# Constant products in TensorE's waits, maxima taken one head at a time, and the bias tables' flips between the turns of tiles

## The chip, the cores and the metric

The kernel runs on one core of a Trainium2 chip. The metric is the device time in microseconds of one execution, from its start to its end. A time of the kernel before is the median of three executions; the profile is of a further execution, which has a time of its own. Numbers of the trace are in microseconds (us) from the first instruction, unless they are marked ns. A few names recur. TensorE (PE) multiplies matrices; VectorE (DVE), ScalarE (ACT) and GpSimd (POOL) do the work by element; SyncE (SP) starts transfers. PEclk is the clock granted to TensorE as a share of full speed: 0.50 is 1.2 GHz and 1.00 is 2.4 GHz.

## The reference

Two transformer blocks in float32, one after the other, over 1024 tokens of width 1024 with 256 context tokens beside them. What bears on this case:

```python
# first block, two layers
h = rms_norm(x, norm_gain[l]) * (1 + scale) + shift          # also for the context tokens
z = h @ w_in[l]                                              # 22 tiles of 128 columns
a_out = global_gqa(aq, ak, av, ak_c, av_c)                   # dense softmax attention, 8 query heads of 64
b_out = pool_branch(bz, pool_w[l], pool_scale[l])
n_out = neighbourhood_attn(nq, nk, nv, nk_c, nv_c, na_rpb[l], rows)   # with a table of relative biases
x = x + gate * (concat(a_out * silu(ag), b_out * silu(bg), n_out * silu(ng)) @ w_out[l])
...
# second block, one layer
z = rmsnorm(x, g_mix) @ w_in
y_fox = softmax(q k^T + c_q - c_k, causal) @ v               # 8 heads of 64
y_rwkv = rwkv7_scan(...)                                     # a recurrence over the tokens
x = x + (gate_fox * (y_fox @ w_o_fox) + gate_rwkv * (y_rwkv @ w_o_rwkv)) @ w_out
x = x + (gelu(u1) * u2) @ w_down                             # u = conv(rmsnorm(x) @ w_up)
x = x + sigmoid(rmsnorm(x) @ w_ple_gate) * (p @ w_ple_up)
```

## The kernel before

Activations lie feature-major in SBUF, tiles of 128 features by 1024 (or 1280, with the context) tokens. A product is made from rounded parts: a weight and an operand are each split into a high and a low part, and three products (`w.hi` x `hi`, `w.hi` x `lo`, `w.lo` x `hi`) are added up in one bank of the accumulators. Weight tiles come one by one into a ring of two, and GpSimd splits each when the tile before it in its slot has been used (`part_weights`, L252 and L254; first two: L230 and L238, or `part_first`, L220 and L222).

The program is a row of sections with a barrier of all engines between them; inside a section each engine has its own list and waits on semaphores. The sections, with their place in the profiled span:

- `opening` and `project` for layer 0 (to 398 us) and layer 1 (1017 to 1329 us): the norm makes the operand tile by tile, k = 0 to 7, and TensorE multiplies two weight tiles with each as it comes (L1719 to L1721); then a chunk at a time. The third weight tile (j == 2) can be split only when the first two are through.
- `attention_operands` (399 to 426, 1330 to 1356 us): TensorE turns 30 tiles of values in 8 groups (L1128), ScalarE copies each group out (L1168); then it flips four bias tables, one a head (L1136), VectorE masks and fills each (L1187, L1190), and GpSimd makes a narrower copy (L1151).
- `pair_attention` (426 to 725, 1356 to 1622 us; with a decay term, "fox", 2747 to 2966 us): two heads (a pair) at a time, queries in blocks of 512. Before a block, its row maxima are found: `maximum(m)` multiplies 128 queries of both heads with up to 512 keys (L836; the decay and the mask are added by L840) into one tile of two banks, and one VectorE reduction takes both heads (L988). `row(b)` turns the negated maxima into a row (L849), ScalarE copies it (L923). Then `scores` (L868, L869), the exponential (L951; L948 in fox), `values` (L880) and `sums` (L889). One list written by a planner, `order`, sets the sequence of all of these for every engine; what stands in it before the first `scores` is done ahead. A maximum's product of the first block alternates between two tiles; of any later block it has one tile (`pg.aux`) and so waits for the reduction before it.
- `neighbour_attention` (728 to 855, 1626 to 1740 us): scores L1260, turns L1271, values L1282.
- `gemm_residual` with `multiply` (to 1013, 1863, and from 3075 to 3172 us) and `gemm_merge` (2974 to 3067 us). With a maker, `multiply` takes k = 0 to 7 as the gated operand comes (`maker.ready`), two weight tiles at once, and then a tile at a time. At its end the squares of x are summed to the mean (L408).
- `branches` (1865 to 2411 us): the second block's projections (L2396 to L2398).
- `rwkv_scan` (2415 to 2702 us): for each of 16 chunks a chain of four outer steps, s = 0 to 3 (L2939 and L2942; L2949, L2955 and L2958; L2965; L2972 and L2976), with ScalarE or VectorE between them. Up to chunk 11 the inner steps of later tiles stand between the outer ones; the outer steps of the last two tiles (chunks 12 to 15) stand alone. Then `rwkv_finish`.
- `feed_forward` (3174 to 3923 us) and `gemm_gated_residual` (to the end).

Where TensorE waits for the maxima's reductions, in the words of the code:

```python
if b >= 1:
    pe.wait_ge(max_done, m)
elif m >= 2:
    pe.wait_ge(max_done, m - 1)
for hh in range(2):
    mm = nc.tensor.matmul(max_tile(m)[:, hh, 0:cw], ...)
```

Of the kernel before, what the change touches and what calls it, by code (L numbers as in the profile page):

```python
# [15 lines left out]
ALU = mybir.AluOpType  # L16
# [5 lines left out]
P = 128  # L22
D = 1024
KD = D // P
# [232 lines left out]
def multiply(nc, pe, w, rhs, acc, chunks, nk, acc_ready, acc_free, n, turns=1, maker=None, beside=None):  # L257
# [11 lines left out]
    if maker:  # L269
        maker.tensor(pe)  # L270
        pe.wait_ge(w.parted, 4)
        pe.wait_ge(acc_free, 2)
        for k in range(nk):
            maker.ready(pe, k)
            for b in range(2):
                for c0, cn in chunks:
                    mm = product(b, c0, cn, k)
                if k == nk - 1:
                    mm.then_inc(acc_ready, 1)
    for b in range(2 if not maker else 0):  # L280
        if b == 0:
            pe.wait_ge(w.half_parted, 1)
# [8 lines left out]
        mm.then_inc(acc_ready, 1)  # L291
    if beside:
# [30 lines left out]
def gemm_store(pg, w_of, n, rhs, z, chunks, nk=KD, func=None, loads=()):  # L323
# [3 lines left out]
    with ExitStack() as st:  # L327
        w = Weights(pg, st, nk)
        acc_ready, acc_free, loaded = pg.sem("acc_ready"), pg.sem("acc_free"), pg.sem("operands_loaded")
        with nc.Block() as block:  # L330
# [9 lines left out]
            def _(pe):  # L340
                multiply(nc, pe, w, rhs, pg.acc, chunks, nk, acc_ready, acc_free, n)
# [19 lines left out]
def gemm_residual(pg, cn, w_of, n, rhs, x, parts, nk, store=None, squares=None, maker_in=None, beside_in=None, x_source=None):  # L361
# [7 lines left out]
    with ExitStack() as st:  # L369
# [9 lines left out]
        with nc.Block() as block:  # L379
# [21 lines left out]
            def _(pe):  # L401
                multiply(nc, pe, w, rhs, pg.acc, chunks, nk, acc_ready, acc_free, n, maker=maker, beside=beside)
                if squares:
                    pe.wait_ge(sq_added, n - 1)
# [281 lines left out]
def pair_attention(pg, cn, pairs, q_cols, totals, ring, beside=None, mask=None, parts=None):  # L686
# [60 lines left out]
    order = [task for at in sorted(tasks) if at < 0 for task in tasks[at]]  # L747
    for e in range(len(exps) + lag + 6):
# [27 lines left out]
    with ExitStack() as st:  # L776
# [40 lines left out]
        with nc.Block() as block:  # L817
            @block.tensor
            def _(pe):
                def maximum(m):  # L820
                    b, qb, i, c0, cw, further = pieces[m]
                    p = blocks[b][2]
                    if m == first_piece[b]:
# [14 lines left out]
                    for hh in range(2):  # L838
# [3 lines left out]
                    mm.then_inc(max_scored, 1)  # L842
# [50 lines left out]
                for kind, j, *i in order:  # L893
                    if kind == "max":
                        maximum(j)
                    elif kind == "row":
                        row(j)
# [60 lines left out]
            def _(dve):  # L958
# [22 lines left out]
                def maximum(m):  # L981
# [3 lines left out]
                    if m == first_piece[b] and b >= 2:  # L985
                        dve.wait_ge(row_made, b - 1)
                    dve.wait_ge(max_scored, m + 1)
                    nc.vector.tensor_reduce(part_max[:, b % 2, j, :, i:i + 1], max_tile(m)[:, :, 0:cw], AX_X, ALU.max,  # L988
                                            negate=True).then_inc(max_done, 1)
                    if i == count - 1 and j == qn // P - 1:  # L990
                        dve.wait_ge(max_done, m + 1)
# [80 lines left out]
def attention_operands(pg, cn, l, mix, na, v_tok, k_twice, k_rest, table, inner, gates_in):  # L1072
# [25 lines left out]
    with ExitStack() as st:  # L1098
# [12 lines left out]
        with nc.Block() as block:  # L1111
# [11 lines left out]
            def _(pe):  # L1123
                for g, (tiles, dst) in enumerate(groups):
# [5 lines left out]
                pe.wait_ge(masks_loaded, 32)  # L1130
                for h in range(NA_HEADS):
# [6 lines left out]
                    mm.then_inc(flipped, 1)  # L1138
                for i in range(2 if gates else 0):
# [60 lines left out]
def neighbour_attention(pg, cn, units, v_of, pooling_in):  # L1200
# [26 lines left out]
    with ExitStack() as st:  # L1227
# [19 lines left out]
        with nc.Block() as block:  # L1247
# [5 lines left out]
            def _(pe):  # L1253
                def scores(i):
                    q, k, pieces, bias, tiles = units[i]
                    if i >= 1:
# [379 lines left out]
def project(pg, cn, l, x, h, mix, na, pool_z, spare, mod, gain_x, gain_c, gates_dram, weights, opened):  # L1636
# [62 lines left out]
    with ExitStack() as st:  # L1699
# [23 lines left out]
        with nc.Block() as block:  # L1723
# [48 lines left out]
            def _(pe):  # L1772
                def norm():
                    for c, (c0, cw) in enumerate(() if opened else BOTH):
# [5 lines left out]
                        mm.then_inc(x_spread, 1)  # L1780
                    pe.wait_ge(parted, 2)
# [8 lines left out]
                for kind, i in order:  # L1790
                    if kind == "norm":
                        norm()
                    elif kind == "gemm":
                        j, c, c0, cw = chunks[i]
                        if c == 0:
                            pe.wait_ge(parted, j + 1)
                        pe.wait_ge(kept, kept_before(j, c))
# [1785 lines left out]
```

## Time and profile before

| | |
|---|---|
| median of three executions | 4059.61 us (4057.88 to 4069.99) |
| profiled execution | 4062.47 us |
| its span, first to last instruction | 4060.7 us |
| TensorE busy | 3622.6 us (89%), 25164 instructions |
| VectorE busy | 1922.8 us (47%) |
| ScalarE busy | 1098.3 us (27%) |
| GpSimd busy | 1641.4 us (40%) |
| mean granted clock of TensorE | 0.937 |

The page of the profile gives each engine's busy time, and the span in 40 equal slices with the busy share and the granted clock in tenths. Its list of waits says for whom an engine sat idle. A row of a timeline has the start, the duration, engine, line, operation, tiles and shape, a count of merged instructions, and in brackets the idle time before it and who ended it. A row of windows has a stretch, and for each engine the busy time and the number of instructions in it.

### The profile page before, as it was taken

Reading aid. Unit: us, or ns where it says so; the run is one execution under the profiler, and the core shown is the slowest. Engines: PE = TensorE matmul, PEld = TensorE weight load, DVE = VectorE, ACT = ScalarE, POOL = GpSimd, SP = SyncE. Lnnn points to the kernel's source line nnn. Section 1 sums busy time; section 2 is a strip of 40 time slices with the busy share of each in tenths; the row PEclk is TensorE's granted clock in tenths of the full one; section 3 lists DMA queues with packets and bytes.
Section 4 is the critical chain, followed back from the end, with each engine's and each line's share of the span. In section 5 each row is a group of like instructions: output and inputs, shape, how many; then the busy total and the mean of one; then the engine's idle time right before and its main releaser. Section 6 shows DMA issues by size and latency. Waiting matters only on the chain. (4 is left out here: it accounts for less than half of the span.)

```text
span 4060.7 us, 58584 instructions
## 1 busy us (share of the span) xinstructions
PE 3622.6 (89%) x25164; PEld 2712.6 (67%) x25164; DVE 1922.8 (47%) x1914; ACT 1098.3 (27%) x1544; POOL 1641.4 (40%) x897
## 2 busy tenths in 40 slices
PE   5999799879899798977999997787888899999988
PEld 4887333668678333766776776764467688888877
DVE  4442566552542565633549204434543562635542
ACT  3223344430223344411245212223410210101120
POOL 1332366442333366443347444402443344444433
PEclk9999799989899799988999999977889899999999
DMA  4012100044111100041211210020032111111111
GB/s 179 32 46 70 52 1 0 15 157 155 58 36 69 26 1 1 15 150 57 90 56 47 98 66 4 4 94 0 1 107 100 42 46 49 52 47 47 52 47 68
DMA packets 93736, 226.85 MB, mean 56 GB/s; under 512 B 28320, under 2 KB 37536, under 8 KB 92592
## 3 DMA queue, kind: packets, MB, share of 16 engines
q1 hardware_dynamic: 76096, 188.75, 13.5%
q10 hardware_dynamic: 17392, 34.48, 2.6%
q8 instruction: 195, 3.19, 0.3%
q14 instruction: 53, 0.43, 0.0%
HBM read 184.36 MB, written 38.83 MB: 55 GB/s over the span
## 5 line engine op out<-in xcount | busy, mean ns | idle before, releaser
L1719 PE MATMUL acc<-h_hi,weights_hi 128*128 128x512 f32 (+1 forms) x928 | 365.9, 394 | 24.6 <-DVE h_lo L1877 18.7
L988 DVE TENSOR_REDUCE part_max<-aux 128x2 f32<-128x856 f32 (+5 forms) x234 | 237.8, 1016 | 224.8 <-PE aux L836 154.8
L1721 PE MATMUL acc<-h_hi,weights_lo 128*128 128x512 f32 (+1 forms) x928 | 340.2, 367 | 0.0
L1720 PE MATMUL acc<-h_lo,weights_hi 128*128 128x512 f32 (+1 forms) x928 | 340.0, 366 | 0.0
L2396 PE MATMUL acc<-h_hi,weights_hi 128*128 128x512 f32 x672 | 274.2, 408 | 25.6 <-DVE h_lo L2674 15.7
L3297 PE MATMUL acc<-h_hi,weights_hi 128*128 128x512 f32 x704 | 276.0, 392 | 12.7 <-DVE h_lo L540 9.2
L3345 POOL TENSOR_TENSOR weights_hi<-weights,ones 128x1024 fp32r<-128x1024 f32 (+1 forms) x66 | 122.5, 1857 | 392.8 <-PE acc L3299 392.8
L3298 PE MATMUL acc<-h_lo,weights_hi 128*128 128x512 f32 x704 | 275.7, 392 | 0.0
L3299 PE MATMUL acc<-h_hi,weights_lo 128*128 128x512 f32 x704 | 275.4, 391 | 0.0
L1891 DVE RECIPROCAL arena<-arena 128x512 f32<-128x512 f32 (+1 forms) x48 | 141.7, 2953 | 263.3 <-ACT arena L1854 263.3
L2398 PE MATMUL acc<-h_hi,weights_lo 128*128 128x512 f32 x672 | 263.5, 392 | 0.0
L2397 PE MATMUL acc<-h_lo,weights_hi 128*128 128x512 f32 x672 | 263.2, 392 | 0.0
L1758 POOL TENSOR_TENSOR weights_hi<-weights,ones 128x1024 fp32r<-128x1024 f32 x42 | 80.4, 1914 | 432.6 <-PE acc L1721 392.5
L951 ACT ACTIVATE probs<-acc 128x1024 f32<-128x1024 f32 (+1 forms) x168 | 168.5, 1003 | 273.5 <-PE acc L869 257.2
L880 PE MATMUL acc<-probs,v_tok 128*64 128x512 f32 (+3 forms) x864 | 232.4, 620 | 2.2 <-DVE inverse L1008 2.2
L1719 PEld LDWEIGHTS acc<-h_hi,weights_hi 128*128 128x128 f32 x928 | 176.4, 190 | 67.3 <-issue 32.0
L1720 PEld LDWEIGHTS acc<-h_lo,weights_hi 128*128 128x128 f32 x928 | 176.5, 190 | 40.7 <-issue 13.5
L836 PE MATMUL aux<-k_twice,q_both_parts 64*128 64x428 f32 (+5 forms) x468 | 120.2, 509 | 89.9 <-DVE part_max L988 42.8
L868 PE MATMUL acc<-q_both_parts,k_twice 128*128 128x512 f32 (+3 forms) x432 | 197.4, 458 | 1.2 <-ACT q_and_shift L923 1.2
L836 PEld LDWEIGHTS aux<-k_twice,q_both_parts 64*128 64x128 f32 x468 | 49.3, 206 | 220.7 <-DVE part_max L988 138.4
L1721 PEld LDWEIGHTS acc<-h_hi,weights_lo 128*128 128x128 f32 x928 | 176.2, 190 | 28.9
L1059 POOL TENSOR_TENSOR total<-total,probs 128x1024 f32<-128x1024 f32 (+1 forms) x72 | 158.7, 2205 | 52.0 <-ACT probs L948 25.9
(460 smaller groups left out, 8435.9 us busy)
## 6 DMA issues: line engine op xcount, KB each, us to landing
weights<-in_w_in SPq DMA_DIRECT2D x44, 512.0 KB, 3.3
weights<-in_w_up SPq DMA_DIRECT2D x43, 512.0 KB, 3.2
arena<-in_w_mod SPq DMA_DIRECT2D x6, 2048.0 KB, 9.6
weights<-in_w_out SPq DMA_DIRECT2D x21, 512.0 KB, 5.3
weights<-in_w_mod SPq DMA_DIRECT2D x4, 2048.0 KB, 26.4
mixer_gates<-arena SPq DMA_DIRECT2D x32, 256.0 KB, 2.0
x_between<-arena ACTq DMA_DIRECT2D x16, 512.0 KB, 3.8
weights<-in_w_gates SPq DMA_DIRECT2D x16, 512.0 KB, 3.3
```

The source lines that it names most:

```text
L868: nc.tensor.matmul(tile[:, hh], twice[:, at], qs[:, p % 2, hh, cols], start=True, stop=False)
L880: mm = nc.tensor.matmul(outs[blk % 2][halves[hh], skip:qn], pairs[p].v(t, hh), probs[:, e % ring, hh, skip:qn], start=i == 0, stop=e == bl ...
L988: nc.vector.tensor_reduce(part_max[:, b % 2, j, :, i:i + 1], max_tile(m)[:, :, 0:cw], AX_X, ALU.max, negate=True).then_inc(max_done, 1)
L1719: nc.tensor.matmul(out, w_hi[:, b, k, :], hi[:, k, cols], start=(k == 0), stop=False)
L1720: nc.tensor.matmul(out, w_hi[:, b, k, :], lo[:, k, cols], start=False, stop=False)
L1721: return nc.tensor.matmul(out, w_lo[:, b, k, :], hi[:, k, cols], start=False, stop=(k == KD - 1))
L2396: nc.tensor.matmul(out, w_hi[:, b, k, :], hi[:, k, at], start=(k == 0), stop=False)
L2397: nc.tensor.matmul(out, w_hi[:, b, k, :], lo[:, k, at], start=False, stop=False)
L2398: return nc.tensor.matmul(out, w_lo[:, b, k, :], hi[:, k, at], start=False, stop=(k == KD - 1))
L3297: nc.tensor.matmul(out, w.hi[:, b, k, :], rhs_hi[:, k, c0:c0 + cols], start=(k == 0), stop=False)
L3298: nc.tensor.matmul(out, w.hi[:, b, k, :], rhs_lo[:, k, c0:c0 + cols], start=False, stop=False)
L3299: return nc.tensor.matmul(out, w.lo[:, b, k, :], rhs_hi[:, k, c0:c0 + cols], start=False, stop=(k == nk - 1))
```

## The change

A function `keep_busy` issues a number of products of a constant tile (`pg.mean`, 128x128 float32) with itself, into a bank that is free at that place. Nothing reads the result. It is called in TensorE's list ahead of waits:

```diff
+def keep_busy(pg, bank, times):
+    for _ in range(times):
+        pg.nc.tensor.matmul(bank[:, 0:P], pg.mean[:], pg.mean[:], start=True, stop=True)
```

| where | products |
|---|---|
| `multiply` with a maker: at its start; before k == 2 | 36; 12 |
| `multiply` without a maker: at its start | 16 |
| `multiply`, before the third weight tile, behind a wait for the first accumulator | 8 |
| `gemm_residual` with squares and no `beside`, before the mean; `feed_forward`, before the mean | 10 |
| `project`, before k = 0: layer 0; layer 1 | 12; 36 |
| `project` and `branches`, before the third weight tile, behind the wait for its accumulator (moved ahead) | 8 |
| `branches`, before k = 0 | 44 |
| `feed_forward`, before k = 0; before the third weight tile | 22; 8 |
| `gemm_gated_residual`, before the first products | 18 |
| `neighbour_attention`, before the second unit's scores | 8 |
| `attention_operands`, behind the second turn | 16 |
| `rwkv_scan`, before each outer step but s = 1 from (chunk 12, s = 3) on: ten places | 3 |
| `pair_attention`, ahead of the first maximum: layer 0; layer 1; fox | 4; 12; 24 |
| `pair_attention`, what is done ahead: each maximum of block 0; of a later block; each row | 2; 4; 5 |
| `pair_attention`, before the first maximum of pairs 1 to 3: first block; fox | 4; 8 |

In `pair_attention` the maxima go one head at a time: each head's product waits for that head's reduction of the tile before, gives its own signal, and VectorE reduces it by itself.

```diff
-                    if b >= 1:
-                        pe.wait_ge(max_done, m)
-                    elif m >= 2:
-                        pe.wait_ge(max_done, m - 1)
                     for hh in range(2):
+                        if b >= 1:
+                            pe.wait_ge(max_done, 2 * m - 1 + hh)
+                        elif m >= 2:
+                            pe.wait_ge(max_done, 2 * m - 3 + hh)
                         mm = nc.tensor.matmul(max_tile(m)[:, hh, 0:cw], ...)
+                        if not further:
+                            mm.then_inc(max_scored, 1)
...
-                    dve.wait_ge(max_scored, m + 1)
-                    nc.vector.tensor_reduce(part_max[:, b % 2, j, :, i:i + 1], max_tile(m)[:, :, 0:cw], AX_X, ALU.max,
-                                            negate=True).then_inc(max_done, 1)
+                    for hh in range(2):
+                        dve.wait_ge(max_scored, 2 * m + hh + 1)
+                        nc.vector.tensor_reduce(part_max[:, b % 2, j, hh, i:i + 1], max_tile(m)[:, hh, 0:cw], AX_X, ALU.max,
+                                                negate=True).then_inc(max_done, 1)
```

In `attention_operands` the eight turns came first and the four flips behind them. Now:

```diff
+                turn(0)
+                turn(1)
+                keep_busy(pg, pg.acc[:, 0], 16)
+                pe.wait_ge(masks_loaded, 32)
+                flip_head(0)
+                flip_head(1)
+                for g in range(2, len(groups)):
+                    turn(g)
+                    if g in (3, 5):
+                        flip_head(g // 2 + 1)
```

## Rows read from the trace of the kernel before

**Rows 1.** The page: TensorE's busy share and granted clock in 40 slices.
```profile
PE   5999799879899798977999997787888899999988
...
PEclk9999799989899799988999999977889899999999
```
**Rows 2.** Span and mean granted clock of the core.
```profile
core 0: 4060.7 us, clock 0.937
```
**Rows 3.** Windows: stretches granted the low clock; busy by engine (count), then PEclk.
```profile
428.00:472.40 44.40, 30.60 (x83) 13.88 (x84) 27.57 (x29) 7.42 (x7) 7.03 (x3) 0.50 0.00 0
1353.00:1383.70 30.70, 18.50 (x53) 9.23 (x54) 18.79 (x21) 7.34 (x7) 5.97 (x10) 0.50 0.00 1
1787.50:1793.30 5.80, 5.75 (x14) 4.50 (x15) 0.00 (x0) 0.00 (x0) 4.13 (x2) 0.50 0.43 126
2667.10:2708.10 41.00, 34.64 (x498) 29.29 (x493) 6.97 (x14) 5.29 (x12) 0.95 (x1) 0.50 0.09 32
2745.70:2793.40 47.70, 30.92 (x102) 19.86 (x103) 22.26 (x26) 10.34 (x13) 7.97 (x4) 0.50 0.00 0
2895.80:2906.10 10.30, 10.30 (x31) 5.54 (x32) 5.67 (x7) 2.93 (x5) 4.70 (x2) 0.50 0.00 0
3168.90:3192.80 23.90, 12.98 (x46) 11.41 (x47) 11.48 (x8) 7.51 (x9) 7.29 (x4) 0.50 0.27 88
```
**Rows 4.** Timeline of PE: float32 products of 128x128 by 128, two instructions each.
```profile
739.51 1.50 PE L1271 MATMUL acc<-inverse_diagonal,probs 128*128 128x128 f32 x12
...
1017.75 4.46 PE L1778 MATMUL aux<-ident,rstd_by_token 128*128 128x128 f32 x20 [1.69 <-PEq L154]
```
**Rows 5.** Windows: a stretch full of such products, and the one behind it.
```profile
1018.50:1021.90 3.40, 3.40 (x18) 3.40 (x17) 0.00 (x0) 0.95 (x2) 0.00 (x0) 0.50 0.85 265
1021.90:1025.30 3.40, 0.31 (x3) 0.12 (x1) 2.65 (x2) 0.94 (x3) 3.27 (x2) 1.00 0.19 46
```
**Rows 6.** Windows of line L951 alone: exponentials begun (x), then PEclk.
```profile
453.70:472.80 19.10, 4.09 (x4) 0.51 0.00 0
558.70:568.30 9.60, 3.05 (x3) 1.00 0.00 0
```
**Rows 7.** Timeline: reductions of block 0, a later maximum's product, a pair's first.
```profile
435.10 1.04 DVE L988 TENSOR_REDUCE part_max<-aux 128x2 f32<-128x856 f32 x1
436.06 1.03 DVE L988 TENSOR_REDUCE part_max<-acc 128x2 f32<-128x848 f32 x1
...
447.25 0.72 PE L836 MATMUL aux<-k_twice,q_both_parts 64*128 64x428 f32 x2 [1.14 <-DVE part_max L988]
...
1406.72 0.46 PE L836 MATMUL aux<-k_twice,q_both_parts 64*128 64x428 f32 x2 [1.41 <-ACT q_and_shift L916]
```
**Rows 8.** PE's waits: who waited for whom, us in total, times, longest us.
```profile
PE aux L836 <- DVE part_max L988: 42.8, 55, 2.2
PE acc L264 <- DVE h_lo L1965: 41.1, 4, 16.5
...
PE acc L2396 <- DVE h_lo L2674: 15.7, 1, 15.7
```
**Rows 9.** Timeline of PE in the scan: one outer step warm, then the chain alone.
```profile
2656.59 0.69 PE L2955 MATMUL acc<-arena 128*64 128x64 f32 x16
...
2674.84 1.12 PE L2939 MATMUL aux<-arena 128*64 128x64 f32 x16 [0.85 <-DVE arena L3031]
...
2677.80 1.12 PE L2955 MATMUL acc<-arena 128*64 128x64 f32 x16
...
2681.49 1.12 PE L2972 MATMUL aux<-arena,token_major 64*64 64x64 f32 x16 [0.67 <-ACT arena L3066]
...
2684.31 1.12 PE L2939 MATMUL aux<-arena 128*64 128x64 f32 x16 [0.85 <-DVE arena L3031]
```
**Rows 10.** Timeline of layer 1's operands: a turn that waits, and the first mask.
```profile
1338.02 2.97 PE L1128 MATMUL aux<-ident,arena 128*128 128x128 f32 x12 [6.19 <-ACT v_tok L1168]
...
1345.21 1.23 DVE L1187 TENSOR_TENSOR arena<-acc,col_mask 128x1024 f32<-128x1024 f32 x1 [6.34 <-PE acc L1136]
```

More of the change, by code:

```diff
@@ L254, in part_weights, with multiply @@
             nc.gpsimd.tensor_tensor(w.lo[:, b], w.raw[:, b], full(w.hi[:, b]), ALU.subtract).then_inc(w.parted, 1)
-def multiply(nc, pe, w, rhs, acc, chunks, nk, acc_ready, acc_free, n, turns=1, maker=None, beside=None):
+def multiply(pg, pe, w, rhs, acc, chunks, nk, acc_ready, acc_free, n, turns=1, maker=None, beside=None):
+    nc = pg.nc
     def product(b, c0, cn, kr):
@@ L401, in _ @@
             def _(pe):
-                multiply(nc, pe, w, rhs, pg.acc, chunks, nk, acc_ready, acc_free, n, maker=maker, beside=beside)
+                multiply(pg, pe, w, rhs, pg.acc, chunks, nk, acc_ready, acc_free, n, maker=maker, beside=beside)
                 if squares:
+                    if not beside:
+                        keep_busy(pg, pg.aux[:, 1], 10)
                     pe.wait_ge(sq_added, n - 1)
@@ L747, in pair_attention @@
     order = [task for at in sorted(tasks) if at < 0 for task in tasks[at]]
+    n_ahead = len(order)
     for e in range(len(exps) + lag + 6):
@@ L822, in maximum @@
                     p = blocks[b][2]
+                    if m == first_piece[b] and p and blocks[b - 1][2] < p:
+                        pe.wait_ge(row_copied, b)
+                        pe.wait_ge(max_done, 2 * m)
+                        keep_busy(pg, pg.aux[:, 0], 8 if own_keys else 4)
                     if m == first_piece[b]:
@@ L891, in sums @@
                     mm.then_inc(summed, 1)
-                for kind, j, *i in order:
+                for at, (kind, j, *i) in enumerate(order):
                     if kind == "max":
+                        if at < n_ahead:
+                            keep_busy(pg, outs[1], first_idle if j == 0 else 2 if pieces[j][0] == 0 else 4)
                         maximum(j)
                     elif kind == "row":
+                        if at < n_ahead:
+                            keep_busy(pg, outs[1], 5)
                         row(j)
@@ L1123, in _, with turn @@
             def _(pe):
-                for g, (tiles, dst) in enumerate(groups):
+                def turn(g):
+                    tiles, dst = groups[g]
                     if g >= 2:
@@ L1129, in _, with flip_head @@
                     mm.then_inc(turned, 1)
-                pe.wait_ge(masks_loaded, 32)
-                for h in range(NA_HEADS):
+                def flip_head(h):
                     pe.wait_ge(placed[h], 32)
@@ L2040, in query_pair @@
                         keys=(k_twice[:, kv, :], k_rest[:, kv, :]))
-        pair_attention(pg, cn, [query_pair(p) for p in range(4)], SEQ + q_ctx * P, [by_head(5), total[:]], 4, by_head(4))
+        pair_attention(pg, cn, [query_pair(p) for p in range(4)], SEQ + q_ctx * P, [by_head(5), total[:]], 4, 12 if last else 4, by_head(4))
     pg.end_section()
@@ L3480, in build @@
         cn = {k: pg.sbuf(stack, k, [P, P]) for k in ("ident", "head_mean", "rot", "mean")}
+        pg.mean = cn["mean"]
         cn["eps"] = pg.sbuf(stack, "eps", [P, 1])
```

41 lines of the change are left out of this document (31 added, 10 removed).

## The prediction

> **What bounds the kernel.** I read the page's slices first. TensorE is busy in nine tenths or more of half the slices, and its granted clock is lowest (7) in slices 5, 14, 27 and 28, in all of which it is busy for only seven or eight tenths [rows 1]. So the kernel is bound by TensorE, and part of what bounds it is its clock. The mean grant is 0.937 [rows 2]; with two levels, 0.50 and 1.00, that is (1 - 0.937) / 0.5 x 4060.7 = 512 us at the low one. Work of TensorE takes twice as long there, so halving it gives back at most half of what TensorE does in those 512 us, less what other engines set.
>
> Next I took windows of the low stretches [rows 3]. There are two kinds. In the starts of attention (428 to 472, 1353 to 1384, 2746 to 2793 us) and of the feed-forward (3169 to 3193 us) TensorE is busy for 54 to 69% and waits between short pieces. In others (1787.5, 2896 us) it has no idle left, works through at 1.2 GHz and pays the full factor of two. The scan's tail (2667 to 2708 us) lies between: 34.64 of 41.0 us, in a chain. In every case the low grant began behind waits and ended after a stretch of unbroken work.
>
> **Would these products hold the clock?** The trace has the same form: float32 128x128 by 128, two instructions each. Twelve took 1.50 us with the clock up, hence 0.11 us an instruction and 0.22 a product; ten took 4.46 us with it down (0.22 and 0.43) [rows 4]. The stretch from 1018.5 us is full of just this form at 0.50, and the next has 1.00, though TensorE is nearly idle in it [rows 5]. So the products count as activity. Their price if exposed: 8 cost 1.7 us warm and 3.4 cold, 36 cost 7.8 and 15.4, 44 cost 9.6 and 18.8, 24 cost 5.2 and 10.2.
>
> One rule speaks against these counts. The Trainium skill ("TensorE: Matmul & The Clock Gate", the section on the back-to-back issue gap) gives 55.6 ns for a 128-column matmul at full clock. By it eight products would fill 0.45 us and cover no wait at all, and the exposed ones below would cost a quarter; the trace's 0.22 us contradicts that for float32, so the sum goes by the row.
>
> **The change, part by part** (negative is time saved).
>
> (a) Starts of attention. Here TensorE and the exponentials pace each other: four exponentials of block 0 took 19.10 us cold (4.78 each), three in the warm middle 9.60 (3.20), a ratio of 0.67 [rows 6]. Before them comes the chain of maxima. In block 0 two tiles alternate and VectorE is the pace: 0.96 us from one reduction of both heads to the next, 1.04 long [rows 7]. Two reductions of half the columns read as much and pay their fixed part twice; no row shows a half alone, so from below I bound that at 0 and from above at 0.2 a piece, and take 0.06, the difference between spacing and duration being small: 12 pieces x 0.06 = 0.7 us. In later blocks a piece is a cold product pair, 0.72 us, and the reduction, in turn; warm the pair takes 0.46, and with heads separate one head's product runs while the other is reduced, so about 1.9 us falls to 1.3. Layer 0: four exponentials -6.3, two later pieces -1.2, split +0.7, leftover products at the very start, which are still cold, +1: about -6, and -7 with the first scores behind them. Layer 1 has a shorter stretch, most of it set by reductions: -1.5. Fox has 48 us at 0.50, two thirds streaming [rows 3], and its decay products (L840) halve too: with the same 0.67 on its last 28 us, -9, and on its maxima -4: -13. Together **-21.5**; bounds -35 and 0.
>
> (b) Between pairs. A pair's first maximum waits for ScalarE's row copy or queries (1.41 us of idle before 1406.72) [rows 7], and then the clock can go down for a stretch without idle, as at 2896 us [rows 3]. I count eight such stretches behind pair changes, 68 us in all. Warm, half would go; the exponentials allow only a third (0.67 again): 68 x 0.33 = -22, less two for stretches that a later wait opens: **-20**; bounds -34 and 0. The new products run in the idle 1.4 us (8 take 1.7, 4 take 0.9), at most +2.
>
> (c) Scan's tail. One chunk alone takes 2684.31 - 2674.84 = 9.47 us cold; an outer step of 16 takes 1.12 against 0.69 warm (0.62) [rows 9]. In it TensorE waits twice, 0.85 and 0.67, together 1.52; three products warm are 0.65, so they vanish in these, but before s = 2 there is no gap and they add 0.65. The gaps are ScalarE's and VectorE's and stay; the other 9.47 - 1.52 = 7.95 are TensorE's: 7.95 x 0.62 + 1.52 + 0.65 = 7.1, so -2.4 a chunk, x 3.6 chunks = -8.6; the finish behind it -2.3; less 15%, since a filled gap may not be enough to keep the clock: **-9.3**; bounds -13 and +8 (all charged cold, four chunks at +2.3 less the small gain of the finish).
>
> (d) The third weight tile. TensorE waits until GpSimd has split it and then five times, 18.9 us in all, the largest 5.75 at 1787.5 [rows 3], goes on cold without idle. Eight products fill the wait: half of 18.9 = 9.5, x 0.9 = **-8.5**. The two waits are only swapped in order; both stand in front of the same product, so that moves nothing. In the merge and in the output product of layer 1 I see no wait before that tile: there the eight are exposed, 2 x 1.74 = **+3.5**, against about 3 that their starts give: **0** net; bounds -9.5 and +3.5.
>
> (e) The other waits: mean before norms (10), norm starts (12, 36, 44, 22), neighbours (8), gated end (18). The longest are not filled: L264 waits up to 16.5 us for h_lo and L2396 15.7 [rows 8], and 44 products end after 9.6. There the clock goes down all the same, and the first k steps wait for h_lo at any clock. What gives is the feed-forward's start (24 us at 0.50, 12.98 busy [rows 3]; about 4.6), means (3.4), neighbours (3): **-11**; bounds -30 and 0.
>
> (f) Operands, layer 1. TensorE's turns wait 6.19 us for ScalarE's copies, and the first mask begins at 1345.21, since flips come behind all turns; VectorE was idle 6.34 us before it [rows 10]. Moved up, the flip can run when its diagonals have landed, near 1339, and the last masks are the section's end: six earlier, less 16 products in TensorE's way and the shared copies: **-4.5**; bounds -6 and +2. Nothing is queued behind the new wait for masks but turns, which wait for ScalarE anyway. In layer 0 the diagonals' own load ends the section: 0.
>
> (g) Maxima one head at a time, in the main phase. 234 reductions become 468. VectorE is half idle and the longer list hides, except where TensorE waits: 42.8 us in 55 waits [rows 8]. For those the first head can start one reduction sooner (-0.3 each at best, -15); against that, queued behind the second head's wait stand scores which ScalarE needs, and each half pays a fixed part. I take **-2**; bounds -10 and +16.
>
> A rule on that fixed part: the Trainium skill ("VectorE: DVE Perf Modes", the cycle table of the errata) gives a read from PSUM 120 + columns cycles at 0.96 GHz, by which a half of 428 columns is 571 ns and a piece costs +0.125 us rather than 0.06. For the whole of 856 columns it gives 1017 ns, and the trace agrees (1.04 us [rows 7]). By it each start would cost 1.5 rather than 0.7 us, 1.6 more for both.
>
> Sum: -21.5 - 20 - 9.3 - 8.5 + 0 - 11 - 4.5 - 2 = -76.8. The profiled execution took 4062.47 us: 3985.7. The median is 2.9 lower, so **3983 us**.
>
> **Rivals**, each from the median of 4059.6.
>
> B, covered. TensorE gets its clock, but its partner sets the pace: exponentials and VectorE in (a) and (b), GpSimd's splitting in (d), ScalarE and VectorE in (c). For: TensorE is idle in a third of the starts [rows 3]. Against: 0.67 was read from a warm middle that has the same partners. Half of the sum: -38, 4022.
>
> C, full gain. All low stretches named go at nearly their whole TensorE work: (a) -35, (b) -30, (c) -12, (d) -9, (e) -20, (f) and (g) -8: -114, 3946.
>
> F, heads apart. Now the two heads' products lie on different rows of the array and take 0.72 us for both. Split by a wait, they run one after the other: +0.3 in each of 55 waits is +16: -61, 3999.
>
> D, slower. The products don't hold the clock and are charged at 0.43 each where they outlast the wait: merges 6.8, scan 8, block-0 maxima 24 x 2 x 0.2 = 9.5, later pieces 5, restarts 3, pair changes 2.5, starts 3: +38, less 4.5 of (f): 4093. It decides only if the clock gives back less than 33 us. Against it: rows 5. For it: the products come in short bursts, and no row shows that such a burst *keeps* a clock, only that a long one raises it.
>
> E, nothing: gains and charges cancel, 4060.
>
> **Chances.** Forecast 0.45, B 0.25, C 0.12, F 0.06, D 0.07, E 0.05. A measurement can tell about 0.3% (12 us) from no change. Faster 0.88, same 0.05, slower 0.07. The range goes from a little past C to above B: 3938 to 4038, which leaves out D, E and the edge of C.
>
> **What would show it.** (a) the slices over 428 to 472 and 2746 to 2793 us at 9 in the clock row, L951's spacing there near 3.3; wrong if the clock is up and the spacing still 4.8 (B). (b) no fully busy stretch at 0.50 behind a pair's first maximum. (c) 7.1 us from one L2939 to the next; 11.8 is D. (d) L1719 behind the third tile at 1.00. (e) the 16.5 us waits still there and still followed by 0.50. (f) first mask near 1339. (g) L988 twice as often at 0.55 us; the waits for it in total under 43 us, over it F. The forecast is wrong above all if the clock still goes down behind filled waits, because eight or four products don't bridge them.

## The result, and the profile after

The changed kernel takes 4008.13 us (median of four executions, 4003.81 to 4027.90), the kernel before 4063.38 in the same comparison: a ratio of 0.9872, 95% interval 0.9849 to 0.9894. A second comparison gave 0.9880 (0.9861 to 0.9898). I use the middle of the two, 0.9876, below: 50 us less. The forecast was 3983, 77 us less: the direction was right, the size half as large again as what came.

The profiled execution has a span of 4010.2 us against 4060.7. The page after, TensorE's busy share and granted clock in 40 slices, and the core's mean grant (lines that answer to [rows 1] and [rows 2]):

```profile
PE   6999999889999899998999997888989999999998
...
PEclk9999799999999999999999999988999999999999
```
```profile
core 0: 4010.2 us, clock 0.968
```

The grant rises from 0.937 to 0.968, so the low level covers (1 - 0.968) / 0.5 x 4010.2 = 257 us in place of 512. Slice 14 has gone from 7 to 9, slices 27 and 28 from 7 to 8; slice 5 (layer 0's start of attention) still has it. Half the low time is gone, and it gave 50 us: about 0.2 us for each us at the low level, less than the third that I had taken for attention.

Where they came from, by section (from the last product of TensorE in one section to the last in the next; in us):

| section | before | after | difference | forecast |
|---|---|---|---|---|
| operands, layer 0 | 30.2 | 32.8 | +2.6 | 0 |
| attention, layer 0 | 296.6 | 292.6 | -4.0 | -7 and a share of (b) |
| neighbours, both layers | 251.2 | 248.5 | -2.7 | -3 |
| output product and mean, layer 0 | 160.8 | 157.1 | -3.7 | in (d), (e) |
| project, layer 1 | 310.1 | 308.4 | -1.7 | in (d), (e) |
| operands and attention, layer 1 | 295.5 | 281.4 | -14.1 | -6 and a share of (b) |
| output product and mean, layer 1 | 123.4 | 118.3 | -5.1 | in (d), (e) |
| `branches` | 547.5 | 547.6 | 0 | in (d), (e) |
| scan and finish | 330.0 | 331.2 | +1.2 | -9.3 |
| attention, fox | 219.3 | 198.4 | -20.8 | -13 and a share of (b) |
| merge and output product | 204.6 | 205.0 | +0.4 | 0 |
| mean, norm, feed-forward | 757.0 | 753.6 | -3.5 | in (d), (e) |
| norm and last product | 132.0 | 133.0 | +1.0 | in (e) |

In these two traces, attention's three starts, pair changes and heads were forecast at -43.5 and gave -32.5 (the -14.1 holds -6.4 for the operands); the scan was forecast at -9.3 and gave +1.2; operands at -4.5 and gave -3.8; what lies outside at -19.5 and gave -15.3. Two places stand out: the scan, which got longer, and layer 0's start, which gave little. Windows of the trace after (stretch, then busy time of TensorE, weight loads, VectorE, ScalarE, GpSimd with their counts, then PEclk) show both:

```profile
432.30:456.20 23.90, 23.90 (x90) 17.31 (x90) 14.79 (x27) 0.96 (x1) 0.00 (x0) 0.50 0.00 1
...
1362.30:1390.50 28.20, 27.97 (x116) 13.91 (x116) 17.32 (x28) 15.70 (x16) 16.01 (x7) 1.00 0.01 1
2637.30:2657.80 20.50, 20.39 (x252) 18.32 (x253) 1.58 (x4) 2.28 (x5) 0.00 (x0) 0.50 0.01 2
2657.80:2674.10 16.30, 15.56 (x324) 13.77 (x324) 3.45 (x7) 2.65 (x6) 0.00 (x0) 1.00 0.01 3
```

In the first and the third TensorE is next to never idle and stays at 0.50, for 23.9 and 20.5 us. In the scan the clock fell at 2637.3, before the first of the products (2643.31). In layer 0 the four products ahead ended at 430.31, TensorE waited 1.31 us more, and the clock fell at 432.3. Behind such a fall the products fill the waits, as meant, but here they don't soon raise the clock: they are work at half speed on the path. The second, layer 1's first exponentials, is the forecast come true: the clock is up and there is next to nothing left to fill.

### The profile page after: what moved, and what is told of

It reads as the page before. It is cut to its first block and busy times, and to the rows that moved or that the text cites. A ratio compares the mean times of both kernels' runs of the same rounds, so it can differ in the third digit from the quotient of the medians.

```text
span 4010.2 us, 61305 instructions
## 1 busy us (share of the span) xinstructions
PE 3736.2 (93%) x26398; PEld 2848.3 (71%) x26398; DVE 1935.0 (48%) x2162; ACT 1099.3 (27%) x1544; POOL 1642.2 (41%) x897
## 3 DMA queue, kind: packets, MB, share of 16 engines
q1 hardware_dynamic: 76096, 188.75, 13.7%
## 5 line engine op out<-in xcount | busy, mean ns | idle before, releaser
L1015 DVE TENSOR_REDUCE part_max<-aux 128x1 f32<-128x428 f32 (+5 forms) x468 | 252.8, 581 | 179.9 <-PE aux L856 130.2
L1799 POOL TENSOR_TENSOR weights_hi<-weights,ones 128x1024 fp32r<-128x1024 f32 x42 | 80.4, 1915 | 430.1 <-PE acc L1762 390.6
L902 PE MATMUL acc<-probs,v_tok 128*64 128x512 f32 (+3 forms) x864 | 223.4, 598 | 2.2 <-DVE inverse L1035 2.2
L890 PE MATMUL acc<-q_both_parts,k_twice 128*128 128x512 f32 (+3 forms) x432 | 188.8, 438 | 1.4 <-ACT q_and_shift L949 1.2
L2496 POOL TENSOR_TENSOR weights_hi<-weights,ones 128x1024 fp32r<-128x1024 f32 x42 | 84.1, 2002 | 231.3 <-PE acc L2443 203.7
L161 PE MATMUL acc<-mean 128*128 128x128 f32 x998 | 151.0, 312 | 27.7 <-PEq L154 16.1
L3401 POOL TENSOR_TENSOR weights_lo<-weights,weights_hi 128x1024 fp32r<-128x1024 f32 (+1 forms) x66 | 172.4, 2612 | 5.2
```

Of the source, the lines that this page charges most:

```text
L890: nc.tensor.matmul(tile[:, hh], twice[:, at], qs[:, p % 2, hh, cols], start=True, stop=False)
L902: mm = nc.tensor.matmul(outs[blk % 2][halves[hh], skip:qn], pairs[p].v(t, hh), probs[:, e % ring, hh, skip:qn], start=i == 0, stop=e == bl ...
L1015: nc.vector.tensor_reduce(part_max[:, b % 2, j, hh, i:i + 1], max_tile(m)[:, hh, 0:cw], AX_X, ALU.max, negate=True).then_inc(max_done, 1)
```

## The experiments

Ratios are to the kernel before, measured beside each. "Products" are the constant ones. "Than the changed kernel" goes by 0.9876, and where it was measured beside the experiment, by 0.9880.

**Heads alone.** The kernel before with the split of the maxima (the second diff of the section on the change) and nothing else.

> The kernel before with the maxima taken one head at a time and nothing else of the change. My theory (the heads' split is nearly neutral, the products carry the gain): block 0's reductions go from 0.955 to 1.03 us a piece, 3 x 12 pieces x 0.075 = +2.7 us less what is idle anyway, the later pieces keep 1.60 to 1.61 us, and the time stays within 4 us of the kernel before (ratio 0.999 to 1.001). Rival H (the split shortens the waits for part_max and carries a good part of the gain): -15 us, ratio 0.996. Rival F (the two heads' products run apart): +16 us, ratio 1.004.

Measured: 0.9998 (0.9986 to 1.0010). The split by itself moves nothing; H and F fall. VectorE's rows of its block 0 (layer 0), and TensorE's waits for these reductions:

```profile
434.49 1.10 DVE L1015 TENSOR_REDUCE part_max<-acc 128x1 f32<-128x428 f32 x2
435.51 1.10 DVE L1015 TENSOR_REDUCE part_max<-aux 128x1 f32<-128x428 f32 x2
```
```profile
PE aux L856 <- DVE part_max L1015: 17.2, 29, 2.2
```

A piece costs 1.02 in place of 0.955 us [rows 7], +0.07 (I had taken 0.06). The waits fell from 42.8 to 17.2 us [rows 8], and yet the time is the same. In this trace layer 0's mix of products worked with next to no idle at 0.50 for much longer behind pair changes than in the trace before:

```profile
485.50:509.40 23.90, 23.90 (x56) 9.31 (x55) 10.06 (x19) 4.68 (x5) 10.43 (x5) 0.50 0.00 0
560.60:581.10 20.50, 20.43 (x47) 7.67 (x48) 8.18 (x15) 4.43 (x5) 10.64 (x5) 0.50 0.00 0
```

Before, the first of these had ended after 6.9 us (486.0) and the second after 3.4 (554.3 to 557.7). Layer 0's attention is 309.1 us in this one profile, against 296.6. The next experiment has the same heads, and its trace shows the same two stretches, 23.9 us from 485.1 and 20.5 from 560.2, and the same 309.1 us. So the split may itself prolong them, which would take back what it saves in waits. It isn't shown: in layer 1 it went the other way (6.9 us at 1417.3 against 13.7 at 1407.6 before), and both traces are of slower executions of their kernels (4068.88 us where the median is 4055.90, and 4061.61 where it is 4050.07). A section's time from one profile is therefore good to no better than 5 to 10 us in attention, and the verdicts here go by the ratios.

**No products at all**, split and flips kept:

```diff
 def keep_busy(pg, bank, times):
-    for _ in range(times):
+    for _ in range(0):
```

> The changed kernel with every count of constant products set to nought: the split heads and the moved flips stay. My theory: layer 1's operands keep their -6 us, layer 0's flips cost 0 to +3, heads +1 to +3: -2 us against the kernel before (ratio 0.9985 to 1.0005), and the granted clock is back at 0.937. Rival (order and heads carry the gain, products only fill): -40 us or more, ratio 0.990.

Measured: 0.9982 (0.9970 to 0.9995), the grant 0.934 in the profiled execution and 0.937 in the mean of twelve. That is 7 us where I expected 2. Against heads alone it is 0.0016, 6.5 us, for the moved flips, part (f); the two intervals overlap, but layer 1's operands, to ScalarE's first work of attention, take 24.5 us here and 30.5 with heads alone. The products carry the rest, 0.9876 against 0.9982: 43 us of the 50.

**None in what attention does ahead:**

```diff
-                            keep_busy(pg, outs[1], first_idle if j == 0 else 2 if pieces[j][0] == 0 else 4)
+                            keep_busy(pg, outs[1], 0)
...
-                            keep_busy(pg, outs[1], 5)
+                            keep_busy(pg, outs[1], 0)
```

> The changed kernel without the products in what attention does ahead (before the first maximum, each maximum and each row); those between pairs and in all other places stay. My theory: layer 0 gets back the 8.6 us that its block of maxima lost (1.80 us a piece falls to 0.95 to 1.03) and loses about 3 in the exponentials behind; layer 1 loses 3, fox 5 to 10 since its maxima and first exponentials run at 0.50 again: 0 to +8 us against the changed kernel. Rival (these products carry most of the gain): +20 to +30 us.

Measured: 0.9904 (0.9884 to 0.9925), some 11 us more than the changed kernel, a little over what I expected and well under the rival. Layer 0 does get its reductions back: 1.02 us a piece, against these rows of the changed kernel, where 2 constant products and the maxima's two hold TensorE at 0.50 and VectorE waits (first two rows, layer 0, 1.81 from one to the next), while layer 1, entered with 12 products and warm, has 1.03:

```profile
437.52 1.11 DVE L1015 TENSOR_REDUCE part_max<-acc 128x1 f32<-128x428 f32 x2 [0.58 <-PE acc L856]
439.33 1.11 DVE L1015 TENSOR_REDUCE part_max<-aux 128x1 f32<-128x428 f32 x2 [0.69 <-PE aux L856]
...
1347.80 1.11 DVE L1015 TENSOR_REDUCE part_max<-aux 128x1 f32<-128x428 f32 x2 [1.81 <-PE aux L856]
1348.83 1.11 DVE L1015 TENSOR_REDUCE part_max<-acc 128x1 f32<-128x428 f32 x2
```

**None in the scan** (`keep_busy(pg, region[0], 0)`):

> The changed kernel without the products in the scan. My theory: the clock is down as the tail is entered and the products cost at the low clock (10.96 and 11.71 us a chunk) what they give back once it is up (7.64): without them the four chunks take about 9.5 each and the tail 36 to 37 us as with them; the time is the same within 2 us. Rival 1 (they gain as forecast): +9 us. Rival 2 (they are a pure charge): -5 us.

Measured: 0.9898 (0.9880 to 0.9916), 9 us more by the middle values, but the intervals of the two kernels overlap, so the ratio leaves open whether the scan's products are worth anything. The tail (chunks 12 to 15) is clearer, since it needs nothing but the trace. Without products it took 37.0 us here and 36.3, 37.0 and 35.6 in the traces before, with heads alone and with no products; with the scan's products 36.7 and 38.7 (the changed kernel twice), and in other kernels of this study that have the same code there 28.3 (none ahead, none between pairs), 31.3 (both heads at once), 33.6 (twelve products) and 35.3 (none outside attention). What differs is the clock: in the two of 28.3 us it is up throughout, in the five others it falls within 1.5 us of chunk 12's beginning, before the first of the scan's products, and rises again after 6.9 to 27.3 us. Windows: none in the scan (first), and the kernel without those ahead in attention (second), which happens to enter warm:

```profile
2639.10:2680.10 41.00, 34.64 (x516) 30.20 (x517) 6.18 (x13) 5.29 (x12) 0.95 (x1) 0.50 0.06 17
```
```profile
2634.20:2662.50 28.30, 27.20 (x572) 24.17 (x572) 4.99 (x10) 4.93 (x11) 0.00 (x0) 1.00 0.01 2
```

Without products the clock fell within 2 us of the same place in all four traces, and stayed down for about 41 us or more. So the scan's products *hold* a clock that is up, all four chunks, and gain 8 us; where it falls before they begin, what is left runs from a gain of about 5 to a cost of about 2. Chunk by chunk in the changed kernel (TensorE, the first outer step of chunks 12, 13 and 14): 10.96 and 11.71 us while it is down, 7.64 behind.

```profile
2637.41 1.12 PE L2989 MATMUL aux<-arena 128*64 128x64 f32 x16 [1.35 <-DVE arena L3081]
...
2648.37 1.12 PE L2989 MATMUL aux<-arena 128*64 128x64 f32 x16
...
2660.08 0.69 PE L2989 MATMUL aux<-arena 128*64 128x64 f32 x16 [0.37 <-DVE arena L3081]
```

**The changed kernel again**, as a base for the next three:

> The changed kernel itself once more, beside the others on this chip, as the base of the comparisons: 0.987 to 0.989 of the kernel before.

Measured: 0.9880 (0.9861 to 0.9898).

**Both heads at once, with all products** (the split undone):

> The changed kernel with the maxima taken for both heads at once again, all constant products kept. The split alone made no difference (ratio 0.9998 with nothing else of the change). My theory: it makes none here either, within 4 us of the changed kernel (0.987 to 0.989 of before). Rival (the split pays only once the clock is up, because then the wait for the reduction is what is left): 8 to 15 us slower than the changed kernel, 0.990 to 0.992.

Measured: 0.9917 (0.9900 to 0.9933), 15 us more than the changed kernel beside it. My theory fell and the rival's size holds: the split, worth nothing alone, is worth about 15 us in the company of the products. TensorE's waits for the reductions, heads together and then split (the changed kernel beside it):

```profile
PE aux L856 <- DVE part_max L1012: 29.8, 43, 1.3
```
```profile
PE aux L856 <- DVE part_max L1015: 11.1, 23, 0.8
```

The split waits 18.7 us less. That this became time is likely and not shown: the two profiled executions are only 1.9 us apart, since the one with both heads happened to have less of the low clock (a grant of 0.971 against 0.965; its scan's tail took 31.3 us against 38.7). What the traces do show is fox's attention, 207.8 in place of 200.8 us; the first block's two are no longer with both heads at once than with the split (293.0 and 261.2 against 293.6 and 263.3). Part (g) was sized at -2 with bounds from -10; with the products it is about -15.

**Twelve products before layer 0's first maximum:**

```diff
-... by_head(5), total[:]], 4, 12 if last else 4, by_head(4))
+... by_head(5), total[:]], 4, 12, by_head(4))
```

> The changed kernel with 12 in place of 4 products ahead of layer 0's first maximum (as layer 1 has). My theory: four of them end before the queries come, the clock goes down at 432 us, and the mix behind it (2 products, 2 maxima's products) works 24 us without a pause at 0.50 and does not raise it; 12 reach over that point, block 0 runs at 1.03 us a piece in place of 1.80 and the whole start is warm: -8 to -12 us against the changed kernel. Rival (the same mix also lets the clock down again): 0 to +2 us.

Measured: 0.9885 (0.9866 to 0.9904): no difference in time, so the 8 to 12 us that I expected did not come. In the trace the step itself went as expected: block 0 runs at 1.02 us a piece at 1.00, and layer 0's attention takes 286.0 against 293.6 us. The gain stands in that profile and not in the ratio. The clock still goes down later, at 454.2 us, among the first exponentials:

```profile
432.00:453.00 21.00, 19.58 (x120) 14.08 (x120) 16.60 (x33) 3.31 (x3) 0.00 (x0) 1.00 0.00 1
454.20:464.40 10.20, 9.51 (x22) 4.37 (x21) 4.58 (x9) 2.05 (x2) 4.70 (x2) 0.50 0.00 0
```

**The scan's products begun one chunk earlier:**

```diff
-                    if t >= n_tiles - 2 and s != 1 and (n, s) > (2 * (n_tiles - 2), 2):
+                    if t == n_tiles - 2 and s == 0 and not ci or (n, s) == (2 * (n_tiles - 2) - 1, 3):
+                        wait_used(pe, n_tiles - 2, inner_steps[-1])
+                        keep_busy(pg, region[0], 6 if s == 0 else 3)
+                    elif t >= n_tiles - 2 and s != 1:
                         keep_busy(pg, region[0], 3)
```

> The changed kernel with the scan's products begun one step earlier: 3 before the last outer step of chunk 11, 6 before chunk 12's first, 3 before its s = 2. My theory: the clock is still up at the entry of the tail if the waits of 1.35 and 0.9 us before it are filled, and all four chunks take 7.6 us in place of 10.96, 11.71, 7.64 and 6.41: -7 us against the changed kernel. Rival (the clock falls all the same, since the idle before chunk 12 is older and is not filled): 4 us more are charged cold, +2 to +4 us.

Measured: 0.9874 (0.9857 to 0.9892); against 0.9880 that is 2 us where I expected 7, and not to be told from none. The tail did what was expected, 29.3 us, all at 1.00, with chunks of 7.64:

```profile
2640.60:2669.90 29.30, 28.20 (x579) 25.00 (x578) 4.94 (x10) 4.92 (x11) 0.00 (x0) 1.00 0.01 3
```

**None between pairs** (`keep_busy(pg, pg.aux[:, 0], 0)` in `maximum`):

> The changed kernel without the products between pairs (8 and 4 before the first maximum of pairs 1 to 3). My theory: without them the clock goes down again behind pair changes and the mix of attention works 3 to 24 us at 0.50 before it rises: 12 to 20 us slower than the changed kernel (0.988 of before), that is 0.991 to 0.993. Rival (pair changes are bridged by the head's split and the products ahead anyway): within 4 us, 0.987 to 0.989.

Measured: 0.9936 (0.9915 to 0.9957), 24 us more than the changed kernel. With the next one this is the largest loss from taking a single part out, and the part costs little (about 0.9 and 1.8 us of products a change). All three attentions have their share: 299.9, 270.6 and 208.3 us in this profile against 293.6, 263.3 and 200.8.

**None outside attention and the scan** (15 places at 0):

> The changed kernel without the products outside attention and the scan (starts of products, third weight tiles, means, norms, neighbours, operands; 15 places). My theory, by the offsets between the traces before and after: -3.4, -1.7, -3.5, -2.4, -2.8 and about -3 for the means are lost again, that is +15 to +17 us, 0.991 to 0.992 of before. Rival (they are mostly charged where h_lo is late anyway): 0 to +5 us.

Measured: 0.9932 (0.9914 to 0.9951), 23 us more. (d) and (e) were forecast at 19.5; the edit also takes out the operands' 16 products, which belong to (f).

The four removals of products, ahead (11), in the scan (9), between pairs (24) and outside (23), add up to 67 us, while all of them taken out together cost 43. So what a part is worth in the company of the others is not its share of the gain.

**All of it mended.** The scan as above but without products before s = 2; layer 0's flips behind all turns again; 12 products ahead in layer 0, 18 in fox; none before the third tile where there is no maker:

```diff
-                    elif t >= n_tiles - 2 and s != 1:
+                    elif t >= n_tiles - 2 and s in (0, 3):
...
-    keep_busy(pg, acc[:, 0], 8)
+    keep_busy(pg, acc[:, 0], 8 if maker else 0)
```

> The changed kernel with what the runs so far suggest: the scan's products from chunk 11 on and none before s = 2; layer 0's flips behind all turns as before; 12 products ahead of layer 0's first maximum; 18 in place of 24 in fox; no 8 products before the third tile where there is no maker. My theory, against the changed kernel: -7 (tail entered warm), -3.5 (0.94 us each before s = 2), -2.5 (flips), -5 (layer 0's start), -1 (fox), -2.5 (exposed products): -20 us, 0.983 of before. Rival (stretches at 0.50 open elsewhere and take it back, as with 12 products alone, which won 7.7 us in their section and nothing in the time): -5 us, 0.987.

Measured: 0.9825 (0.9811 to 0.9840), 3984.44 us: 21 us less than the changed kernel. Single mends were too small to be told in a ratio; together they are clear, and near the 20 us that their sections had let me expect. The tail takes 25.3 us, 6.62 a chunk. In layer 0 the clock still goes down. TensorE before and in that stretch: the wait, and the windows before and behind 454.2 us.

```profile
452.59 0.97 PE L856 MATMUL aux<-k_twice,q_both_parts 64*128 64x424 f32 x2 [0.68 <-DVE part_max L1015]
```
```profile
450.30:454.20 3.90, 3.17 (x12) 1.86 (x12) 3.31 (x6) 1.02 (x1) 0.00 (x0) 1.00 0.00 0
454.20:474.70 20.50, 19.81 (x53) 8.45 (x53) 6.85 (x13) 5.11 (x6) 9.41 (x4) 0.50 0.00 1
```

One idle of 0.68 us in a stretch that is busy for 3.17 of 3.90 us, and then 20.5 us at 0.50 with next to no idle.

**Three products in that wait too:**

```diff
+                        elif at < n_ahead + 14 and order[at - 1][0] == "max":
+                            keep_busy(pg, outs[1], 3)
                         maximum(j)
```

> The kernel e12_all_four_mended with 3 more products before each second maximum among the first tasks behind what attention does ahead, where TensorE waits 0.68 us for part_max between scores (452.59 us of e12's trace) and the clock goes down at 454.2 for 20.5 us without idle. My theory: the low stretch comes from these waits; filled, it does not open in layer 0, and the section takes 5 to 7 us less, with 1 or 2 in fox: 3978 us, 0.981 of before. Rival (the mix of attention at that place counts too little anyhow, waits or not: the clock goes down all the same and the 3 products are charged cold): 0 to +3 us against e12.

Measured: 0.9797 (0.9781 to 0.9813), 3976.37 us. That is 11 us less than the last one by the ratios (8 by the medians) and 81 less than the kernel before. The edit applies to all three attentions, not to the one wait alone. In layer 0 the clock stays up through the whole start, and its attention falls from 287.3 to 278.0 us; fox, where I expected 1 or 2, shows nothing (196.9 and 197.2). The window of that start, and the page's clock row:

```profile
450.00:475.00 25.00, 24.56 (x113) 12.25 (x111) 15.56 (x27) 14.84 (x15) 13.34 (x6) 1.00 0.00 1
```
```profile
PEclk9999999999999999999999999999999999999999
```

## Why the prediction was right, and where it was wrong

**The sum.** -76.8 was forecast and the two traces differ by 50.4. Of the 26 us that are missing, attention has 11.0 and the scan 10.5; what lies outside has 4.2 and the operands 0.7. The time, 4008 us, lies between the forecast (3983) and rival B (4022), by the number nearer to B. But B's cause, a partner that sets the pace where the clock is up, isn't what is missing: where the clock is up the exponentials follow, as under (a), and what is missing was lost where it is down. Rival C, 3946, and E, 4060, fall by the time.

**What bounds it, and the mechanism.** Right. Without products the kernel is back at a grant of 0.937 and 0.9982 of before; with them the low time halves. Rival D's condition, products that don't keep a clock, doesn't hold in general (the tail stays at 1.00 for 28.3 us), but its price does appear where the clock is down first: 10.96 and 11.71 us a chunk, where D said 11.8.

**(a) Starts.** The warm pace was read well. Exponentials begun in layer 1's start (clock up) and in layer 0's (clock up for only part of it), trace after: one in 2.56 us, against one in 5.12. Forecast was a spacing near 3.3 warm, and 4.8 if B were true.

```profile
1362.30:1390.50 28.20, 11.35 (x11) 1.00 0.01 1
454.50:480.10 25.60, 5.38 (x5) 0.70 0.00 1
```

Fox, with -20.8 for (a) and (b), came out as foreseen. Layer 0 failed. The step that failed is "leftover products at the very start, which are still cold, +1". The four products of the very start run with the clock up and end before the queries come (the first maximum waits another 1.31 us), the clock goes down at 432.3, and from then on the two products before each of block 0's maxima are charged at the low level: eight pieces start 1.80 to 1.81 us apart where it had been 0.955. From the first reduction to the last the block takes 18.15 us against 10.50, 7.7 more. The sum priced only the first few. D's term "block-0 maxima 9.5" was near that number; I had hung it on the wrong condition, a clock that never rises, where one that falls at the block's beginning is enough.

**(b) Pair changes.** -20 forecast, 24 when taken out: the right size, with the reservation that the removals overlap.

**(c) The scan.** The step that failed is "-2.4 a chunk, x 3.6 chunks": it takes the clock to be up in nearly the whole tail, with only 15% off "since a filled gap may not be enough to keep the clock". Filled gaps did keep it; what I didn't ask is the clock at the entry. In the trace after it is up only in the last 16.3 of the tail's 36.7 us, and scan and finish came out at +1.2 in place of -9.3. The trace before had the answer, since its low stretch begins at 2667.10 [rows 3], in chunk 12, before the first place with products. They begin behind the fall, and the clock comes back only after 20.5 us (27.3 in the changed kernel's other trace). The size of the mechanism was right: -8.6 forecast for a tail held up, 36.3 to 28.3 = -8.0 measured; a chunk 7.64 against 7.1. Part of that difference is that three products (six instructions) put off the next step by 0.87 us where nothing waits (from 2664.47, the row below, to 2665.34), not by 0.65; leaving out those before s = 2 took 1.02 off a chunk.

```profile
2664.47 0.94 PE L161 MATMUL acc<-mean 128*128 128x128 f32 x6
```

**(d) and (e).** -19.5 forecast; -15.3 by sections, 23 when taken out. Right in sum. The low stretches at the third weight tiles before (912.7, 1062.9, 1786.5, 1912.8, 3216.7) have no counterpart after. The merge and the output product behind it came out at +0.4, as the exposed eights and their starts were forecast to cancel. `branches` gave nothing: its wait for h_lo is shorter only because 44 products stand in its place (15.7 [rows 8] to 5.7), and the product goes on when h_lo is there.

**(f) Operands.** Layer 1: -6.4 against -4.5; the first mask begins at 1330.56, 14.7 us earlier in a trace that was 8.3 ahead at the section's start. To ScalarE's first work of attention it is 30.5 us in both traces with the old order and 23.9 to 26.6 in all twelve with the new one. Layer 0 failed on "nothing is queued behind the new wait but turns, which wait for ScalarE anyway". There the diagonals come late, the turns queue behind the flip that waits for them, and the section's end is +2.6. Not all of that is the order: the diagonals also landed 0.9 us later. From their landing to the section's end it is 7.2 to 9.4 us in the four traces with the old order here and 8.8 to 11.3 in the ten with the new one.

```profile
417.51 3.78 PE L1164 MATMUL acc<-diagonals,flip 128*128 128x512 f32 x4 [4.48 <-DMA diagonals<-in_na_rpb]
421.08 1.53 PE L1156 MATMUL aux<-ident,arena 128*128 128x128 f32 x8
```

**(g) One head at a time.** The term was mis-sized: -2 forecast, nothing alone and about -15 beside the products. It isn't a sum of its own. My explanation, that a shorter wait of TensorE pays only once its cold stretches are gone, fits both ratios and isn't shown; that the split itself prolongs cold stretches where there are no products (heads alone) would fit them too. Rival F falls: with heads alone the waits for reductions shrank and no time was added.

**The rule on the issue gap.** By the 55.6 ns that the Trainium skill gives ("TensorE: Matmul & The Clock Gate", "Wait — 56ns, not 53.3ns?") eight products would have been, by estimate, 0.45 us long; its section on the back-to-back issue gap has about 81 ns for a stream of weight load and matmul, which would make them 0.65. The trace agrees with neither for a float32 product: its two instructions start 0.112 us apart each with the clock up (the middle of 924 such gaps in the trace after), 0.22 a product and 1.8 for eight, where the sum had 1.7.

**The rule on VectorE.** By the 120 + columns cycles of the Trainium skill ("VectorE: DVE Perf Modes", cycle table of the errata) a half is estimated at 571 ns. The trace agrees for one instruction (mean 581 ns over 468 of several widths, page after), but a piece of two takes 1.02 to 1.03 us from start to start, not 1.14. The extra is 0.07 a piece, nearer to the 0.06 read from the rows than to the rule's 0.125.

## What to carry to other kernels

Products that fill TensorE's waits hold its clock; they are cheap while it is up and a charge while it is down. So look first at where the clock falls in the trace, and put the first of them before that point, not at the first wait that is easy to reach. Short pauses can matter: filling those of about 0.7 us among attention's first scores was worth 8 to 11 us. And parts depend on each other: the split was worth nothing alone and 15 us beside the products, and the removals add up to more than the whole. So try the parts together as well as alone.

## What the runs showed of the hardware

- TensorE can be next to without idle for 20.5 to 23.9 us and still be granted 1.2 GHz. The stretches of the trace after and of heads alone held many small products: one operand on 64 of 128 rows (the maxima), 64x64 (the scan), 64 output columns (values). But full ones stood among them, in the one at 432.3 even 60 of 90 instructions of the constant product. In all fourteen traces, every stretch of over 6 us at 0.50 in which TensorE is nearly always busy (over 93%) lies in attention or the scan, and none in the sections of 128x128x512 products. A run of 24 instructions of the constant product alone, in contrast, began at layer 1's start at 1342.07, and the clock rose at 1347.1. That "busy" in the trace and what the grant follows are not the same is shown; which property of a product counts is not, no run varied it alone.
- The Trainium skill ("TensorE: Matmul & The Clock Gate", what is actually happening) says that activity releases the throttle. The run of constant products at layer 1's start agrees. With the trace's busy time as the measure of activity the mixed stretches above contradict it.
- The length of such a stretch isn't fixed: in the changed kernel's two traces the clock is low from 432.3 for 23.9 and 20.5 us, and in the scan's tail for 20.5 and 27.3. Executions of one kernel differ along with their mean grant: of 22 of the kernel before, measured side by side, the fastest took 4047.57 us at 0.939 and the slowest 4065.81 at 0.935. With intervals of about 0.002 to each side of most of these ratios, a gain of under 8 us in one section can't be told.
